# Gated product stored from GpSimd's queue, two more copy buffers, pooling sums thinned out, a later statistic, and a folded weight written by two engines

## The reference

```
u = rms_norm(h, g_mix);  z = u @ w_in                  # 5 x 1024 columns
a = z_val * sigmoid(z_gate)                            # the gated product
a = depthwise conv, 31 taps, over tokens (a) + b_dw
y_conv = silu(layer_norm(a, ln_g, ln_b)) @ w_conv_out
p = z_pool: per group of 256 channels, mean over a window of 2, 4, 8 or 16 tokens, minus p
y_pool = ((per-group p @ w_pool) * pool_scale) @ w_pool_out
merged = sigmoid(z_gA + b) * y_conv + sigmoid(z_gB + b) * y_pool
h = h + merged @ w_o
v = rms_norm(h, g_ffn);  h = h + (silu(v @ w_ffn_gate) * (v @ w_ffn_up)) @ w_ffn_down
out = rms_norm(h, g_final)[without the meta tokens]
```

## Time and profile before

| what | us |
|---|---|
| three runs | 1042.4, 1043.03, 1020.64; median 1042.4 |
| profiled execution, its own time | 1021.39 |
| its span on the slowest core (core 5) | 1019.8 |
| spans of the eight cores | 1013.9 to 1019.8 |
| PE busy | 972.2 (95%) |
| DVE, ACT, POOL busy | 423.1, 293.5, 154.8 |
| DMA | 105.81 MB, mean 104 GB/s |

### The profile page before, as it was taken

How to read it: one execution, slowest core, us unless ns; L and a number is a source line. 1 busy time by engine, 2 the same in 40 slices (tenths; PEclk the granted TensorE clock), 3 DMA queues, 4 the chain that set the end, 5 groups by cost and what they waited for, 6 DMA issues and landing times.

```text
span 1019.8 us, 14701 instructions; the slowest of 8 cores (1013.9 to 1019.8 us)
## 1 busy us (share of the span) xinstructions
PE 972.2 (95%) x5176; PEld 473.2 (46%) x5176; DVE 423.1 (41%) x614; ACT 293.5 (29%) x487; POOL 154.8 (15%) x208
## 2 busy tenths in 40 slices
PE   3999999997979999999999999999999999999996
PEld 1645544552424444444444444444444444444485
DVE  4556996533267422322557321211212211242554
ACT  2653134434685112112244311111111111121121
POOL 3141101110391000000366011011000000000000
PEclk9999999997999999999999999999999999999999
DMA  9705677868294222111969344554222003312122
GB/s 214 217 3 84 121 198 177 227 156 195 42 186 108 52 31 31 25 26 22 260 268 241 49 75 80 92 99 70 41 42 38 15 1 123 125 72 94 83 84 83
DMA packets 44231, 105.81 MB, mean 104 GB/s; under 512 B 5760, under 2 KB 18176, under 8 KB 41600
## 3 DMA queue, kind: packets, MB, share of 16 engines
q0 software_dynamic: 20192, 47.20, 26.5%
q1 hardware_dynamic: 23968, 57.68, 17.4%
HBM read 115.80 MB, written 21.04 MB: 134 GB/s over the span
## 4 chain that ended last, share of the span: by engine, by line
PE 84%; DMA 4%; SPq 4%; DVE 3%; ACT 3%; issue 2%; POOL 0%; DVEq 0%; ACTq 0%; POOLq 0%
PE ps L364 82%; SPq L194 4%; DMA ad<-aT 2%; PE ps L678 1%; DMA xb<-xp 1%; DMA rep<-ad 1%; DVE uT L391 1%; DVE s L378 1%; DVE sqx L378 1%; ACT weff L375 1%; ACT cell L375 0%; ACT sqx L375 0%; ACT ps L375 0%; DVE h2b L391 0%; ACT L375 0%
## 5 line engine op out<-in xcount | busy, mean ns | idle before, releaser
L364 PE MATMUL ps<-uT,wslot 128*128 128x416 bf16 (+6 forms) x1536 | 297.0, 350 | 8.9 <-DVE uT L391 5.2
L364 PE MATMUL ps<-vT,wslot 128*128 128x512 bf16 x1408 | 304.4, 379 | 0.0
L364 PEld LDWEIGHTS ps<-uT,wslot 128*128 128x128 bf16 x1536 | 150.0, 99 | 152.3 <-issue 24.5
L364 PEld LDWEIGHTS ps<-vT,wslot 128*128 128x128 bf16 x1408 | 137.7, 98 | 167.0 <-issue 1.6
L378 DVE TENSOR_TENSOR fT<-ps,sgf 128x512 bf16<-128x512 f32 x88 | 60.7, 691 | 229.1 <-PE ps L364 229.1
L364 PE MATMUL ps<-fT,wfd 128*128 128x512 bf16 (+1 forms) x880 | 153.2, 337 | 0.0
L375 ACT ACTIVATE sgf<-ps 128x512 f32<-128x512 f32 x88 | 52.5, 597 | 241.8 <-PE ps L364 234.9
L364 PEld LDWEIGHTS ps<-fT,wfd 128*128 128x128 bf16 x880 | 86.1, 98 | 67.8 <-issue 1.7
L364 PE MATMUL ps<-cell,wslot 128*128 128x512 bf16 x512 | 114.8, 379 | 0.0
L391 DVE SCALAR_TENSOR_TENSOR zt<-zt,ps 128x512 f32<-128x512 f32 x64 | 44.0, 687 | 112.9 <-PE ps L364 110.8
L375 ACT ACTIVATE zt<-ps,hb 128x512 f32<-128x512 f32 x64 | 43.9, 688 | 140.2 <-PE ps L364 140.2
(11 more groups left out here) (75 smaller groups left out, 589.5 us busy)
## 6 DMA issues: line engine op xcount, KB each, us to landing
rep<-ad SPq DMA_DIRECT2D x128, 129.5 KB, 5.4
wslot<-w_in POOLq DMA_DIRECT2D x40, 256.0 KB, 6.3
h1d<-h1b SPq DMA_DIRECT2D x4, 2048.0 KB, 9.5
h2b<-h1d SPq DMA_DIRECT2D x4, 2048.0 KB, 12.7
h1b<-xr SPq DMA_DIRECT2D x3, 2048.0 KB, 19.2
out<-h2b SPq DMA_DIRECT2D x3, 2048.0 KB, 8.2
wslot<-w_ffn_gate POOLq DMA_DIRECT2D x22, 256.0 KB, 4.9
wslot<-w_ffn_up POOLq DMA_DIRECT2D x22, 256.0 KB, 4.8
```

What stands on the lines that cost most here:

```text
L364: S.op(PE, lambda e: e.matmul(out, lhsT=lhsT, rhs=rhs, start=start, stop=stop), [lhsT, rhs], [out], signal=stop if signal is None else signal)
```

## The change

There are five edits. (1) The stores of `a_out` are issued on POOL's queue in place of SP's. (2) There are six `rep` buffers; chunk 7 has two of its own, which lie over `aT` and over `s1`/`s2`, and its `im2col` stands before `conv(6)` in place of after it. `bg` is emptied before, so that `s1` and `s2` are done with. (3) `vg` takes one pooling sum after each piece, not two. (4) `Bm(0,0)` and `Bm(0,1)` move from before `conv(7)` to behind it, so that three gate tiles stand between `conv(7)` and `ln_stat`, where one stood. The `zt` buffers are handed out in plain order. (5) In `fold` the second half of the columns is copied by DVE, the first by ACT as before.

```diff
-           enumerate((z, z + 4 * RWP * 2, oB + 6 * EXT * 4, oB + 7 * EXT * 4))]
+           enumerate((z, z + 8 * RWP, oB + 6 * EXT * 4, oB + 7 * EXT * 4, z + 24064, z + 32384))]
...
-    rep_sem = [dsem(f"d_rep{i}") for i in range(4)]
+    rep_sem = [dsem(f"d_rep{i}") for i in range(6)]
...
-            pump(2)
+            pump(1)
         a_out(c, 3 * HP, HE)
         release(f"gate{c}", f"val{c}")
...
-        S.dma(SP, ad_sem[2 * (c % 2) + h], a_d.ap()[c][:, :, lo:hi], aT[c % 2][:, :, lo:hi], xw=[("ad", c, h)])
+        S.dma(POOL, ad_sem[2 * (c % 2) + h], a_d.ap()[c][:, :, lo:hi], aT[c % 2][:, :, lo:hi], xw=[("ad", c, h)])
...
-        return g % 2 + (2 if g // 2 in (1, 3, 5) else 0)
+        return g % 2 + (4 if g // 2 == KC - 1 else 2 * (g // 2 % 2))
...
-        if c < KC - 1:
-            im2col(c)
+        if c == KC - 1:
+            pump(len(bg))
+        im2col(c)
...
-    zfree = collections.deque(list(range(13, NZT)) + [11, 12] + list(range(11)))
+    zfree = collections.deque(range(NZT))
     conv(6)
-    im2col(7)
...
-    for b in range(2):
-        Bm(0, b)
-        pump(2)
     conv(7)
     pump(len(bg))
...
-                act(weff[:, 2 * g + ki, h * 512:(h + 1) * 512], ps[:], AF.Copy)
+                dst = weff[:, 2 * g + ki, h * 512:(h + 1) * 512]
+                if h:
+                    cp(DVE, dst, ps[:])
+                else:
+                    act(dst, ps[:], AF.Copy)
...
     for g in range(4):
         wps_scale(g)
+    Bm(0, 0)
+    Bm(0, 1)
     Bm(0, 2)
```

## The result

The changed kernel takes 1008.5 us (median of four runs; 1008.0 without the one of 1031.8; the profiled execution reads 1007.67, its span is 1006.1). The ratio to the kernel before is 0.988, 95% interval 0.985 to 0.991: 1.2% faster, within the 2% that were called no change. The forecast of 1008.7 was made for executions like the profiled one and lies 1.0 us above it.

The account below looks back on a forecast made before the run. PE's own work was taken to bound the kernel (84% of the span), so only its stops count. Gains 4.2 + 3.0 + 5.5 = 12.7 us from the profiled 1021.4 gave 1008.7 us, range 1002 to 1030.

Parts of the forecast that it names:

- (a): One pooling sum a piece in vg: PE's three waits for aT go; gain 4.2 us, bounds 1.2 and 4.2.
- (b): Stores on POOL's queue, own chunk 7 buffers: shorter wait around conv(6); gain 3.0 us, bounds nothing and 10.3.
- (c): After conv(7): three tiles before the statistic, eight fold copies on DVE; gain 5.5 us, bounds 0.4 and 8.0.
- What bounds the kernel: PE's own work is 84% of the span, so only what stops PE counts.
- The later burst: Pooling sums returning after conv, 9.6 us with running sums against conv's 3.64; costed at nothing, margin 1.9 us.
- T: Start of conv(5), 228.03 us in the profile before; the prediction's times for stores, copies and taps count from it.
- The clock: Around conv(6): PE's clock probably falls again in the wait; 32 matmuls had taken 3.60 us, against 3.64 for 64.
- signs of being wrong: Stores landing after 10 us, later aT waits, PE waiting for DVE's weff in fold, or a wait before conv(7).
- The rules: DVE locking out GpSimd's DMA descriptors adds nothing; another queue saving only issue time would make the gain 1.55 us.
- the third rival: Stores starved on POOL's queue, kernel slower: gain gone at a landing of 20 us; chance 0.05.
- Places changed: Rival: waits around conv(6) only swap and DVE's copies hold fold; 1014 to 1019.8 us, chance 0.18.
- Both in time: Rival: taps land in under 7 us and the clock stays up; 999 to 1004 us, chance 0.15.

Follow-up runs that it names:

- u_pump: The changed kernel with two pooling sums after each piece again: 1012.6 us, ratio 0.991 to the kernel before.
- cw5: The changed kernel with five tap buffers in place of three: 1000.4 us, ratio 0.978 to the kernel before.
- u_sp: The changed kernel with the stores of the gated product back on SP's queue: 1010.4 and 1012.0 us, ratio 0.990 to the kernel before.
- u_rep: The changed kernel without chunk 7's own buffers, its copies issued after conv(6) into the first two: 1008.5 us, ratio 0.985 to the kernel before.
- cw5_rep: cw5 without chunk 7's own buffers, its copies issued after conv(6) into the first two: 1000.6 us, ratio 0.979 to the kernel before.
- u_bm: u_rep with Bm(0,0) and Bm(0,1) before conv(7) again: 1009.1 us, the one time that counts.
- u_fold: The changed kernel with all 16 fold copies on ACT again: 1012.7 and 1013.4 us, no ratio.
- o_store: The kernel before with only the stores moved to POOL's queue: 1019.4 us, ratio 0.997 to the kernel before.

## Why the prediction was right, step by step

**The number** is closer than its parts. Core 5 before and core 3 after, the slowest ones, differ by 13.7 us: 4.6 in (a), 1.4 in (b), where 3.0 was forecast, 2.8 + 3.8 = 6.6 in (c), where 5.5 was, and 1.2 ahead of `conv(0)`, where the means of the two kernels are equal. That these add up to within 1.0 us of the 12.7 is in part luck, and so is the 0.2 us between 1008.7 and the median of four.

**What bounds the kernel** stood as read: the parts outside the four of the table moved by 0.2 us in 840.

**(a) One pooling sum a piece**: 4.2 forecast, 4.5 measured, and undone by u_pump alone. The later burst cost nothing, as the margin worked out had it: PE has no wait for `aT` on any core.

**(b) Stores on POOL's queue.** The gain was forecast at 3.0 us and is 4.1 in the mean (17.2 to 13.1), but 1.4 between the slowest cores (17.6 to 16.2). The mechanism was right: the copies' wait gives way to one for the taps of group 13 between groups 12 and 13. Two sizes in it were off, and in opposite directions.
- *The store.* I took 8 us to landing, between rows for other transfers. The changed kernel's landed in 4.4 (first part) and 3.2 (second part) in the median. These are its DMA issues from 95 to 245 us, to be held against the earlier trace rows:

```profile
rep<-ad SPq DMA_DIRECT2D x128, 129.5 KB, 5.2
ad<-aT POOLq DMA_DIRECT2D x8, 312.0 KB, 4.4
cw<-cw POOLq DMA_DIRECT2D x16, 128.0 KB, 9.5
ad<-aT POOLq DMA_DIRECT2D x8, 208.0 KB, 3.2
```

  So SP sent the first of chunk 6's sixteen copies at T − 12.6, and not at T − 9 (9.7 us earlier than before, where some 6 were forecast), and the last at T − 3.3, and not at T + 3; the forecast that they would come next at T + 8.5 was wrong, as cw5 shows. It did not follow from its own row either: 2.2 us behind the last issue would be T + 5.2, which is in time. The same store took 6.7 us from SP's queue in the earlier trace rows. But in u_sp, where only its queue is another, it took 4.3 from 165 to 245 us (median of five), against 3.0 there in the changed kernel (four). So most of the 6.7 was not the queue's doing. The rest of the difference may come from the sixteen copies directly ahead of it or from the kind of queue; no run separates them.
- *The taps.* I took their landing from the earlier trace rows, 8.8 us after an issue at T + 2.5. On the slowest core they were issued at 225.45, T + 3.2, and landed 9.2 us later. POOL's timeline on core 3 shows the first part:

```profile
223.72 0.70 POOL L194 DMA_DIRECT2D ad<-aT  x1 [4.94 <-DVE aT L378]
224.31 1.23 POOL L194 DMA_DIRECT2D wslot<-w_pool_out  x2
225.45 0.62 POOL L194 DMA_DIRECT2D cw<-cw  x1
226.50 0.54 POOL L194 DMA_DIRECT2D cw<-cw  x1 [0.43 <-issue]
```

  The load of taps (the first `cw` row) no longer waits for PE (1.33 us in the earlier trace rows), but stands behind a store that waits for DVE: the queue that the store was moved to has its own customers. I had counted these issues and not the 0.7 us that they cost the taps. A wait of 7.3 us on this core and 3.2 to 6.1 on the others came of it, for 4 to 6 forecast.
- *The clock.* It was forecast to fall again, and it fell on six of the eight cores, all but 2 and 7. Core 3, then core 7, whose wait was 3.87 us (windows of two us; the clock is third from the end):

```profile
230.00:232.00 2.00, 0.00 (x0) 0.00 (x0) 2.00 (x3) 0.50 (x1) 0.00 (x0) 0.50 0.86 95
236.00:238.00 2.00, 2.00 (x24) 0.72 (x16) 0.00 (x0) 1.06 (x2) 0.00 (x0) 0.50 1.05 317
```

```profile
230.00:232.00 2.00, 2.00 (x34) 0.91 (x27) 0.70 (x1) 1.07 (x2) 0.00 (x0) 1.00 1.11 291
```

  On core 3 group 13 ran at 1.2 GHz in 3.60 us and the tiles behind it lost another 0.8 (14.7 for 13.9); on core 7 it ran at 2.4 GHz in 1.91. So a wait of 7.3 us costs 9.8, which is why the slowest core won less than the mean. The length of the wait alone does not tell what the clock does: core 5 waited no longer than core 7, and its clock read 0.51 from 228 to 230 us. PE on core 5, then on core 7:

```profile
229.42 3.60 PE L678 MATMUL ps<-rep,cw 128*32 128x512 bf16 x32 [3.82 <-DMA cw<-cw]
229.77 1.91 PE L678 MATMUL ps<-rep,cw 128*32 128x512 bf16 x32 [3.87 <-DMA cw<-cw]
```

**Chunk 7's own buffers** were costed at nothing, and u_rep and cw5_rep find nothing.

**(c) The statistic and the fold**: forecast 5.5 us, measured 3.4 + 3.0 = 6.4. P was to end 43.9 us after `conv(7)` and ended at 42.4 on every core. The statistic comes out as worked (u_bm: 2.1), the copies as worked (u_fold: 4.4 for 4.1). What I took off for the load of `w_pool_out` was not due on these cores. Counted from core 5, on which the forecast was made (46.3 us), P is 1.5 us shorter than forecast, and 1.2 of that is the clock: `P` ran its 58 matmuls in 12.95 us where 57 had taken 14.15 in the earlier trace rows, and the clock, 0.96 over that stretch in the earlier trace rows, is 1.00 now. One of the signs of being wrong did show: PE waits for DVE's `weff` in `fold`, 0.34 to 0.71 us on cores 0, 2 and 5. ACT's copies come later still, and P ends at 42.4 us there too. Core 2, PE:

```profile
276.01 1.02 PE L364 MATMUL ps<-wslot,wslot 128*128 128x512 bf16 x4 [0.67 <-DVE weff L385]
```

**The rules.** That DVE's two-input sums don't hold up the transfers of POOL's queue is borne out twice, in o_store too, where DVE is as busy as before; the starved stores of the third rival are refuted: of the changed kernel's stores none took over 8.9 us to land. The reading by which only the issue time of two DMAs is saved would have given (b) 1.55 us; it is 4.1, and 9.7 where the taps don't bind. The place in the queue is what counts, not the issue: 9.2 us on core 3, as u_sp shows.

**The rivals.** Places changed: the slowest core came near it in (b), with 16.2 for 17.6, but (c) held. Both in time: it needs the taps before T + 5.5, and they never came before T + 8.6. Its price, 7 to 10 us for (b), is what cw5 then measured when they did: 17.2 − 7.1 = 10.1.

## What to carry to other kernels

Where a wait is to be removed, list all that the waiting instruction needs and when each was asked for, not only the releaser that the profile names; here the copies ended their wait at T + 11.0 and the taps had landed at T + 11.3, and with the taps out of the way the same edit is worth 9.7 us and not 4.5. A load asked for when its buffer comes free, a few us before its use, is a wait in hiding; one or two more buffers, where 2 KB lie idle, are the cheapest edit in this study. And two engines that share copies must be costed as rows of instructions: eight to DVE gained 4.4 us, and twelve lost 4.3 of them again.

## What the runs showed of the hardware

- The same 208 KB store landed 6.7 us after its issue on SP's queue in the kernel before, 4.3 on that queue in u_sp, and 3.0 on GpSimd's in the changed kernel (medians of four or five, 165 to 245 us). The taps' 128 KB loads on GpSimd's queue took 7.5 us in the kernel before and in u_sp, with the stores on SP's (95 to 245 us), 9.5 in the changed kernel and 9.6 in o_store, with the stores on theirs.
- One wait of 7.3 us halved the clock for all of group 13 and a little after it (9.8 us in all). Of two waits as long as each other in the same execution, 3.82 us on core 5 and 3.87 on core 7, the first halved it and the second did not; on core 4 of the kernel before it fell after 2.78 us (32 matmuls in 3.57 us for 1.91). No length of wait that is safe can be read from this.
- The cores of one execution differ by up to 5.7 us in this one part (10.5 to 16.2), and that alone makes most of the spread of their spans, 998.7 to 1006.1. In cw5, where the wait is gone, the spans lie between 994.8 and 998.9.
